# Projection phase: the gate projection split into three steps early in a group, and the newest convolution tap written by ScalarE out of PSUM

## The chip, the cores and the metric

One core of a Trainium2 chip runs the kernel. TensorE, VectorE, ScalarE and GpSimd each work through their own instruction queue in order, SyncE issues transfers, and semaphores tie the queues together. The metric is the device time of one execution, in microseconds (us).

## The reference

One inference step of a one-layer streaming encoder: 4096 prompt frames and 8 streams of 16 frames, model width 1024. What bears on the change is the first half of the mixer:

```
proj = rmsnorm(x) @ w_in                      # 3080 columns
x_lru, y_lru, qkv, z, b_logit, a_logit = columns of proj
xc    = causal_conv(x_lru, 4 taps) + lru_cb   # out[t] = sum over j of x[t-3+j] * w[j]
qkv_c = silu(causal_conv(qkv, 4 taps))
out_a = rglru(xc) * gelu(y_lru)               # gates r, i are sigmoids of two small matmuls on xc
beta  = sigmoid(b_logit)                      # 4 columns, one for each head
g     = -exp(a_log) * softplus(a_logit + dt_bias)
```

The gated delta rule, the output projection and a mixture of experts follow. The change doesn't touch them.

## The kernel before

`project_phase` handles 512 tokens (a group) at a time: eight groups of prompt tokens, the middle six in a loop, and a ninth of 128 tokens for the streams. Channels lie on the partitions, tokens along the free axis. The product runs in fp16 halves: each of 24 chunks of 128 columns is 8 x 3 matmuls of 128x512 into one of four PSUM banks (`pP`, L364).

`sequence()` writes down one list of steps, and every engine walks the same list and does its own share of each step. So a step that an engine waits in holds up all later steps of that engine. The steps:

- Y, X, Q, Z with a number: a chunk. TensorE makes it; ScalarE reads it from PSUM. Y (gelu) and Z (silu) are finished so. For X (4 chunks) and Q (12 chunks) ScalarE copies the bank into `win` (L465), and VectorE runs the 4-tap convolution: carry in (L617), a first tap as a product (L620 for X, with the bias; L622 for Q), carry out (L623), three multiply-adds (L626).
- S: silu of a finished Q on ScalarE, and its store. G, R, O: the gates of the recurrence (two matmuls `pG` on an X chunk, ScalarE functions, VectorE arithmetic), the scan, and the store.
- B: the 8 gate columns. TensorE does 96 small matmuls into `pB` (L388). VectorE adds the time bias (L664, `asum`). ScalarE takes the sigmoid, absolute value, exponential and logarithm with three function-table loads (L507 to L512). VectorE, which waits for that, ends with L668 and L670.
- D, E, H, T prepare the next group: VectorE spreads the row scales on a diagonal (D, L558), TensorE sums it over a matrix of ones (E, L347, `pR`), VectorE scales the eight blocks of `xT` (H, L568), ScalarE and VectorE cut them into fp16 halves (T: `h_hi` L423, `h_lo` L574). The next group's Y0 needs each of the halves. N takes the squares of the next tokens on ScalarE (L417).
- P: one of 60 pieces of expert weights for the later phase. A piece comes in by a transfer (256 KB), ScalarE rounds it (L435, `halves`), VectorE takes the remainder (L586), and a transfer writes it out (256 KB). SyncE issues, for each piece in list order, the write and then the load of the piece six places later. The six middle groups and a part of the eighth carry pieces; the first carries the splitting of `w_in` (`w_hi`, `w_lo`), chunk by chunk in the order of `wblocks`.

Before the change, B stands after Q9, D after the first piece behind Q10, and E after Q11 ahead of Z0. From Q3 on each chunk has three pieces.

Of the kernel before, what the change touches and what calls it, by code (L numbers as in the profile page):

```python
# [22 lines left out]
D = 1024  # L23
# [80 lines left out]
def sequence():  # L104

    free = iter(range(PER_GROUP))
    p = lambda n=1: [("P", next(free)) for _ in range(n)]
    w = iter([("W", k) for k in range(KD)])  # L110
    out = [("Y", 0)] + p() + [next(w), ("X", 0)] + p() + [next(w), ("Y", 1)] + p() + [next(w), ("X", 1), ("G", 0)] + p()
    out += [next(w), ("Y", 2)] + p(2) + [next(w), ("X", 2), ("R", 0), ("G", 1)] + p() + [next(w), ("Y", 3)] + p(2)
    out += [next(w), ("X", 3), ("O", 0), ("R", 1), ("G", 2)] + p() + [next(w), ("Q", 0)] + p()
    out += [("O", 1), ("R", 2), ("G", 3)] + p() + [("Q", 1)] + p() + [("S", 0), ("O", 2), ("R", 3)] + p()
    out += [("Q", 2)] + p(2) + [("S", 1), ("O", 3)] + p()
    tokens = {3: 0, 4: 1, 6: 2, 7: 3}
    for m in range(3, QC):
        out += [("Q", m)] + p() + [("S", m - 1)] + ([("N", tokens[m])] if m in tokens else [])
        out += [("B", 0)] * (m == 9) + [("D", 0)] * (m == 10) + [("E", 0)] * (m == 11) + p(2)
    out += [("Z", 0)] + p(2) + [("S", QC - 1)] + p(4) + [("Z", 1)] + p(3) + [("H", k) for k in range(4)] + p(3)  # L120
    out += [("Z", 2)] + [("H", k) for k in range(4, KD)] + [("T", k) for k in range(KD)] + [("Z", 3)] + p(4)
    assert next(free, None) is None and next(w, None) is None
    return out


def project_phase(nc, T, gb, cols):
# [6 lines left out]
    with ExitStack() as ctx:  # L133
# [51 lines left out]
        def col(name, n=0, w=1):  # L185
# [2 lines left out]
        last = f"Z{ZC - 1}"  # L188
        pe_names = [n for a, b in seq if a in "YXQZGB"
                    for n in ([f"{last}.{k}" for k in range(KD)] if f"{a}{b}" == last else (f"{a}{b}",))]  # L190
        act_names = [f"{a}{b}" for a, b in seq if a in "YXQZGRSB"]
        dve_names = [n for a, b in seq if a in "XGRQB" for n in (("Ba", "B") if a == "B" else (f"{a}{b}",))]
        pe_did = Steps(sem("project_pe"), pe_names)
        act_did = Steps(sem("project_act"), act_names)
        dve_did = Steps(sem("project_dve"), dve_names)
# [6 lines left out]
        h_did = Steps(sem("h_dve"), [f"L{k}" for k in range(KD)])  # L202

        wblocks = [(column[a] + m * P, P) for a, m in chunks]
        wblocks.insert(number["Q", 9] + 1, (IN - 2 * HEADS, 2 * HEADS))
        block_of = {c: wblocks.index((column[c[0]] + c[1] * P, P)) for c in chunks}
        block_of["B", 0] = number["Q", 9] + 1
        w_split = sem("w_split")
        w_hi_ready = sem("w_hi_ready")
        weights_in = [sem(f"weights_in{n}") for n in range(2)]  # L210
# [127 lines left out]
        def _(pe):  # L338
# [11 lines left out]
            def group(g, nt, following, first=False):  # L350
                N = nt * P
                for kind, m in seq:
# [17 lines left out]
                    elif kind == "E" and following:  # L370
                        spread(g + 1, following)
                    elif kind == "G":
                        if first and m == 0:
                            pe.wait_ge(gates_in, 16 * 4 * LC)
                        pe.wait_ge(*dve_did.at(f"X{m}", g))
                        pe.wait_ge(*act_did.at(f"G{(m - 1) % LC}", g, back=int(m == 0)))
                        for b in range(2):
                            ins = nc.tensor.matmul(pG[b][:, 0:N], gates[:, b, m, :], cv[:, m, 0:N], start=True, stop=True)
                        ins.then_inc(*pe_did.did(f"G{m}"))
                    elif kind == "B":  # L380
                        if first:
                            pe.wait_ge(w_split, block_of["B", 0] + 1)
                        pe.wait_ge(*dve_did.at("B", g, back=1))
                        pe.wait_ge(*act_did.at("B0", g, back=1))
# [25 lines left out]
        def _(act):  # L410
# [27 lines left out]
            def group(g, nt, stream, following, first=False, pieces=0):  # L438
# [5 lines left out]
                for kind, m in seq:  # L444
# [15 lines left out]
                    elif kind in "XQ":  # L460
# [4 lines left out]
                        nc.scalar.activation(window(c, 3, stream), shaped(pP[number[kind, m] % NPB][:, 0:N], stream),  # L465
                                             ACT.Copy, scale=PROJ).then_inc(*act_did.did(f"{kind}{m}"))
                    elif kind == "G":
                        act.drain()
                        act.wait_ge(*pe_did.at(f"G{m}", g))
# [24 lines left out]
                    elif kind == "Z":  # L494

                        act.wait_ge(*pe_did.at(f"{last}.{KD - 1}" if m == ZC - 1 else f"Z{m}", g))
                        slot = (QC + m) % 2
                        act.wait_ge(qo_out[slot], g * 128 + ((QC + m) // 2 + 1) * 16)
                        nc.scalar.activation(qo[:, slot, 0:N], pP[number[kind, m] % NPB][:, 0:N], ACT.Silu,
                                             scale=PROJ).then_inc(*act_did.did(f"Z{m}"))  # L500
                        act.drain()
                        store(QC + m, qo[:, slot, 0:N], qo_out[slot])
                    elif kind == "B":

                        act.wait_ge(*pe_did.at("B0", g))
                        act.wait_ge(*dve_did.at("Ba", g))
                        nc.scalar.activation(gb[:, bass.ds(g * GT, nt), 0:HEADS], pB[:, 0:nt, 0:HEADS], ACT.Sigmoid, scale=PROJ)  # L507
# [4 lines left out]
                        nc.scalar.activation(alog1[:, 0:nt], aexp[:, 0:nt], ACT.Ln, bias=1.0).then_inc(*act_did.did("B0"))  # L512

            for s in qo_out + halves_out:
                act.sem_inc(s, 16)
# [34 lines left out]
        def _(dve):  # L550
# [38 lines left out]
            def group(g, nt, stream, following, first=False, pieces=0):  # L589
                N = nt * P  # L590
                kept = carry_s if stream else carry
                for kind, m in seq:
# [10 lines left out]
                    elif kind in "XQ":  # L603
# [7 lines left out]
                        if c >= 8:  # L611
                            dve.wait_ge(*act_did.at(f"S{c - 8}", g))
                        elif c < 4:
                            dve.wait_ge(*act_did.at(f"S{QC - 4 + c}", g, back=1))
                        else:
                            dve.wait_ge(*pe_did.at(f"G{m}", g))
# [21 lines left out]
                    elif kind == "R":  # L638
# [12 lines left out]
                        else:  # L651
# [8 lines left out]
                    elif kind == "B":  # L660
                        dve.wait_ge(*pe_did.at("B0", g))
                        dtb = col("dtb", 0, HEADS).unsqueeze(1).to_broadcast([P, nt, HEADS])
                        neg = nea[:, :].unsqueeze(1).to_broadcast([P, nt, HEADS])
                        nc.vector.scalar_tensor_tensor(asum[:, 0:nt], pB[:, 0:nt, HEADS:], PROJ, dtb, ALU.mult, ALU.add  # L664
                                                       ).then_inc(*dve_did.did("Ba"))
                        dve.drain()
                        dve.wait_ge(*act_did.at("B0", g))
# [1651 lines left out]
```

## Time and profile before

| | |
|---|---|
| median of three runs | 3588.89 us (3588.49 to 3590.18) |
| profiled execution | 3602.5 us, span 3600.4 us |
| busy share: TensorE, VectorE, ScalarE | 86%, 59%, 43% |
| mean granted TensorE clock | 0.935 |
| matmuls of L364 in the projection phase | first 26.4 us, last 1284.7 us |
| one loop group, Y0 to Y0 | about 153 us |

The profile puts each engine's busy time and each idle stretch, with the event that ended it, on one time axis. The busy share mixes phases with different limits, so the projection phase is read by itself, and in it the group whose successor's Y0 starts at 632.12 us.

### The profile page before, as it was taken

The page shows a single profiled execution, that of the slowest core. Times are in us where ns is not written, and L with a number is a line of the kernel's source. Part 1 is how long each engine was busy: PE and PEld are TensorE (multiplying, and loading weights), DVE is VectorE, ACT ScalarE, POOL GpSimd, SP SyncE. Part 2 cuts the span into 40 slices and gives each one's busy share as a digit, 9 for nine tenths or more (in the row PEclk, how much of TensorE's full clock was granted, in tenths as well). Part 3 has the DMA queues.
Part 4 walks back from the last instruction along what each step waited for, and adds up shares of the span by engine and source line. Part 5 has one row for each costly group of instructions (what it writes and reads, how often), then busy time and mean ns, then how long its engine had stood idle before and what let it go on. Part 6 is the DMA issues. An engine that isn't in the chain of part 4 may idle for free. (4 is left out here: it accounts for less than half of the span.)

```text
span 3600.4 us, 65633 instructions
## 1 busy us (share of the span) xinstructions
PE 3106.1 (86%) x18226; PEld 1840.1 (51%) x18227; DVE 2124.0 (59%) x5319; ACT 1551.4 (43%) x3036; POOL 787.4 (22%) x1002
## 2 busy tenths in 40 slices
PE   7998898989889955999999999996799999999900
PEld 3443443434344555777777777664355555555500
DVE  5776867768687644676777776664333333333367
ACT  6565766657666522444444444441122222222222
POOL 0000000000000012455445554441111111111154
PEclk9999999999999966999999999998799999999955
DMA  5567769687785244545554454441677879984288
GB/s 157 159 218 275 270 237 321 216 314 256 244 296 203 86 128 116 153 137 154 150 154 134 138 156 138 129 118 56 212 257 249 284 242 320 321 276 155 99 312 312
DMA packets 497880, 733.44 MB, mean 204 GB/s; under 512 B 93425, under 2 KB 243537, under 8 KB 497361
## 3 DMA queue, kind: packets, MB, share of 16 engines
q1 hardware_dynamic: 414464, 497.94, 43.4%
q10 hardware_dynamic: 54288, 146.56, 10.4%
q0 software_dynamic: 28864, 86.09, 6.8%
q8 instruction: 85, 1.39, 0.2%
q14 instruction: 179, 1.46, 0.1%
HBM read 459.52 MB, written 270.92 MB: 203 GB/s over the span
## 5 line engine op out<-in xcount | busy, mean ns | idle before, releaser
L364 PE MATMUL pP<-h_hi,w_hi 128*128 128x512 f16 (+1 forms) x1728 | 628.2, 368 | 46.2 <-DVE h_lo L574 34.7
L364 PE MATMUL pP<-h_lo,w_hi 128*128 128x512 f16 (+1 forms) x1728 | 627.0, 367 | 0.0
L364 PE MATMUL pP<-h_hi,w_lo 128*128 128x512 f16 (+1 forms) x1728 | 625.7, 367 | 0.0
L1956 PE MATMUL ebank<-w_halves,rowsT_hi 128*128 x1568 | 486.5, 382 | 2.3 <-DVE rowsT_lo L2027 1.3
L626 DVE SCALAR_TENSOR_TENSOR cv<-win,cols_sb,cv 128x512 f32<-128x512 f32 (+1 forms) x432 | 305.4, 707 | 35.0 <-issue 0.4
L586 DVE SCALAR_TENSOR_TENSOR halves<-stage,halves 128x512 f16<-128x512 f32 x384 | 249.8, 685 | 94.3 <-ACT halves L435 94.0
L1956 PE MATMUL ebank<-w_halves,rowsT_lo 128*128 x784 | 299.4, 382 | 0.0
L364 PEld LDWEIGHTS pP<-h_hi,w_hi 128*128 128x128 f16 x1728 | 172.4, 100 | 244.2 <-issue 32.5
L435 ACT ACTIVATE halves<-stage 128x512 f16<-128x512 f32 x384 | 229.2, 621 | 107.9 <-DMA stage<-in_raw 75.6
L364 PEld LDWEIGHTS pP<-h_lo,w_hi 128*128 128x128 f16 x1728 | 172.4, 100 | 194.7 <-issue 23.3
L364 PEld LDWEIGHTS pP<-h_hi,w_lo 128*128 128x128 f16 x1728 | 172.2, 100 | 187.1 <-issue 10.5
L328 POOL TENSOR_TENSOR ss<-ss,eps 128x4 f32<-128x4 f32 (+1 forms) x9 | 3.7, 414 | 1153.3 <-ACT gy L417 1141.8
L1978 PE MATMUL ebank<-w_halves,guT_hi 128*128 x784 | 250.4, 381 | 2.4 <-DVE guT_lo L2033 2.4
L1956 PEld LDWEIGHTS ebank<-w_halves,rowsT_hi 128*128 128x128 f16 x1568 | 154.3, 98 | 183.1 <-issue 9.4
L1918 POOL DMA_INDIRECT rows<-h,idx x98 | 96.8, 988 | 687.7 <-PE ebank L1945 682.3
L2038 DVE SCALAR_TENSOR_TENSOR gu<-ebank,sil 128x256 f32<-128x256 f32 x98 | 41.6, 425 | 297.7 <-ACT sil L1997 297.7
L1997 ACT ACTIVATE sil<-ebank 128x256 f32<-128x256 f32 x98 | 37.6, 384 | 328.5 <-PE ebank L1956 328.5
L2043 DVE TENSOR_SCALAR yb<-ebank 128x512 f32<-128x512 f32 x98 | 67.8, 692 | 174.5 <-PE ebank L1978 174.5
L1978 PE MATMUL ebank<-w_halves,guT_lo 128*128 x392 | 149.3, 381 | 0.0
L2027 DVE SCALAR_TENSOR_TENSOR rowsT_lo<-ebank,rowsT_hi 128x512 f16<-128x512 f32 x196 | 126.4, 686 | 16.9 <-ACT rowsT_hi L1992 10.9
L1478 POOL DMA_INDIRECT table<-tid,offs x66 | 69.7, 1057 | 304.1 <-DVE offs L1730 278.3
L2001 ACT ACTIVATE guT_hi<-ebank 128x256 f16<-128x256 f32 x98 | 37.6, 384 | 224.7 <-ACTq L2011 223.6
(353 smaller groups left out, 6442.1 us busy)
## 6 DMA issues: line engine op xcount, KB each, us to landing
stage<-in_raw SPq DMA_DIRECT2D x384, 256.0 KB, 4.5
split<-halves SPq DMA_DIRECT2D x384, 256.0 KB, 4.3
w_halves<-split SPq DMA_DIRECT2D x32, 2048.0 KB, 11.3
y<-yb ACTq DMA_DIRECT2D x98, 512.0 KB, 7.2
ft<-mixin SPq DMA_DIRECT2D x33, 1280.0 KB, 8.3
mixin<-qo ACTq DMA_DIRECT2D x128, 256.0 KB, 3.9
w_halves<-split SPq DMA_DIRECT2D x32, 1024.0 KB, 6.1
xr<-in_x SPq DMA_DIRECT2D x33, 512.0 KB, 5.2
```

The lines of the kernel that those rows point to most:

```text
L364: ins = nc.tensor.matmul(pP[n % NPB][:, 0:N], w[:, k, c0:c0 + P], h[:, k, 0:N], start=(k + i == 0), stop=(k == KD - 1 and i == 2))
L435: nc.scalar.activation(halves[i % NHALF][:, 0, :], stage[:, i % NRAW, :], ACT.Copy, scale=W_SCALE).then_inc(hi_done, 1)
L586: nc.vector.scalar_tensor_tensor(halves[i % NHALF][:, 1, :], stage[:, i % NRAW, :], W_SCALE, halves[i % NHALF][:, 0, :], ALU.mult, ALU.sub ...
L626: ins = nc.vector.scalar_tensor_tensor(dst, window(c, j, stream), cw(j), dst, ALU.mult, ALU.add)
L1478: pool.indirect_dma_start(T["table"], bass.IndirectOffsetOnAxis(ap=offs[k][:, 0:1], axis=0), tid[:, 0:1], None).then_inc(ids_out, 16)
L1918: pool.indirect_dma_start(xb[p][:, :], None, T["h2"], bass.IndirectOffsetOnAxis(ap=idx[q][:, 0:1], axis=0)).then_inc(rows_in[p], 16)
L1956: ins = nc.tensor.matmul((M0, M1)[p][:, :], x[p][:, k, :], w[:, bass.ds(s, 1), k, half, :].rearrange("p a n -> p (a n)"), start=(k + i == ...
L1978: ins = nc.tensor.matmul((OA, OB)[h][:, :], g[p][:, k, :], down.rearrange("p a n -> p (a n)"), start=(k + i == 0), stop=(k == FE // P - 1 ...
L1997: nc.scalar.activation(sil[p][:, :], (M0, M1)[p][:, 0:FE], ACT.Silu, scale=PROJ).then_inc(*did(n))
L2027: nc.vector.scalar_tensor_tensor(part(xl), (TA, TB)[h][:, :], H_SCALE, part(xh), ALU.mult, ALU.subtract).then_inc(*did(n))
L2038: nc.vector.scalar_tensor_tensor(gu[p][:, :], (M0, M1)[p][:, FE:2 * FE], PROJ, sil[p][:, :], ALU.mult, ALU.mult).then_inc(*did(n))
L2043: nc.vector.tensor_scalar(yb[p][:, 512:], OB[:, :], OUT, None, ALU.mult).then_inc(*did(n))
```

## The change

Three things. First, B becomes three steps and moves from behind Q9 into the first half of the group. B (TensorE's 96 matmuls) stands after X1; U (VectorE's bias) after G1; V (ScalarE's functions) after G3; F (VectorE's end) after R3. The sigmoid is now a tanh with halved scale (V), made into a sigmoid by one more VectorE product in F. Second, ScalarE reads each X and Q bank twice: once into `win` as before, and once with the newest tap's weight into `cv` (Identity with a per-partition scale, and for X a per-partition bias). VectorE's first tap is gone; three multiply-adds remain. Those weights are scaled once at the start. Third, E moves behind Z0 and its two pieces. D stays.

```diff
-    out = [...] + [next(w), ("X", 1), ("G", 0)] + p()
+    out = [...] + [next(w), ("X", 1), ("B", 0), ("G", 0)] + p()
...
-        out += [("B", 0)] * (m == 9) + [("D", 0)] * (m == 10) + [("E", 0)] * (m == 11) + p(2)
-    out += [("Z", 0)] + p(2) + [("S", QC - 1)] + p(4) + [("Z", 1)] + ...
+        out += [("D", 0)] * (m == 10) + p(2)
+    out += [("Z", 0)] + p(2) + [("E", 0)] + [("S", QC - 1)] + p(4) + [("Z", 1)] + ...
...
-        wblocks.insert(number["Q", 9] + 1, (IN - 2 * HEADS, 2 * HEADS))
+        wblocks.insert(number["X", 1] + 1, (IN - 2 * HEADS, 2 * HEADS))
...
# ScalarE, X and Q
-    nc.scalar.activation(window(c, 3, stream), shaped(pP[...][:, 0:N], stream),
-                         ACT.Copy, scale=PROJ).then_inc(*act_did.did(f"{kind}{m}"))
+    made = pP[number[kind, m] % NPB][:, 0:N]
+    nc.scalar.activation(window(c, 3, stream), shaped(made, stream), ACT.Copy, scale=PROJ)
+    if 4 <= c < 8:
+        act.wait_ge(*pe_did.at(f"G{c - 4}", g))
+    nc.scalar.activation(cv[:, c % 4, 0:N], made, ACT.Identity, scale=col("cw", 4 * c + 3),
+                         bias=col("cb", m) if kind == "X" else 0.0).then_inc(*act_did.did(f"{kind}{m}"))
...
# ScalarE, B becomes V
-    act.wait_ge(*dve_did.at("Ba", g))
-    nc.scalar.activation(gb[...], pB[:, 0:nt, 0:HEADS], ACT.Sigmoid, scale=PROJ)
+    act.wait_ge(*dve_did.at("U0", g))
+    nc.scalar.activation(gb[...], pB[:, 0:nt, 0:HEADS], ACT.Tanh, scale=0.5 * PROJ)
...
# VectorE, X and Q: the waits for S and G go, and
-    nc.vector.tensor_scalar(dst, window(c, 0, stream), cw(0), None, ALU.mult)
     nc.vector.tensor_copy(kept[:, c], new)
-    for j in range(1, 4):
+    for j in (2, 1, 0):
...
# VectorE, F
+    beta = gb[:, bass.ds(g * GT, nt), 0:HEADS]
+    dve.wait_ge(*act_did.at("V0", g))
+    nc.vector.tensor_scalar(beta, beta, 0.5, 0.5, ALU.mult, ALU.add)
```

VectorE in a loop group, from Q9's convolution to Q11's, before (`halves` is a piece, `rg<-ident_sb,rs` is D):

```order
L626 SCALAR_TENSOR_TENSOR cv<-win,cols_sb,cv 128x512 x3
...
L664 SCALAR_TENSOR_TENSOR asum<-pB,cols_sb 128x16
...
L668 SCALAR_TENSOR_TENSOR aabs<-asum,alog 128x16
...
L670 TENSOR_TENSOR gb<-aabs,nea 128x4x4
...
L617 COPY win<-carry 128x3
L622 TENSOR_SCALAR cv<-win,cols_sb 128x512
L623 COPY carry<-win 128x3
...
L558 TENSOR_TENSOR rg<-ident_sb,rs 128x512
```

and now the place where F stands, between R3 (`oa<-oa,gy`) and Q2's convolution:

```order
L655 TENSOR_TENSOR oa<-oa,gy 128x512
...
L666 TENSOR_SCALAR gb<-gb 128x4x4
L667 SCALAR_TENSOR_TENSOR aabs<-asum,alog 128x16
...
L669 TENSOR_TENSOR gb<-aabs,nea 128x4x4
...
L593 SCALAR_TENSOR_TENSOR halves<-stage,halves 128x512
...
L618 COPY win<-carry 128x3
L620 COPY carry<-win 128x3
L623 SCALAR_TENSOR_TENSOR cv<-win,cols_sb,cv 128x512 x3
```

The three gate instructions have left the stretch between Q9 and D, and the product between the two small copies is gone from all 16 convolutions.

ScalarE in a loop group, from the last gate function of G3 to the next silu, before:

```order
L477 ACTIVATE th<-rg,sp 128x512
L435 ACTIVATE halves<-stage 128x512
...
L465 ACTIVATE win<-pP 128x512
...
L491 ACT_TABLE_LOAD
L491 ACTIVATE qo<-cv 128x512
```

and now, with V ahead of the piece and the second pass behind the copy of Q1:

```order
L481 ACTIVATE th<-rg,sp 128x512
...
L511 ACTIVATE gb<-pB 128x4x4
L512 ACTIVATE aabs<-asum 128x16
L514 ACTIVATE aexp<-aabs 128x16
L516 ACT_TABLE_LOAD
L516 ACTIVATE alog<-aexp 128x16
...
L466 ACTIVATE win<-pP 128x512
L469 ACTIVATE cv<-pP,cols_sb 128x512
...
L495 ACT_TABLE_LOAD
L495 ACTIVATE qo<-cv 128x512
```

One table load stands in V, where B had three; the load ahead of the next silu after B falls away too, since ScalarE then stays with silu from Q2's step to the group's end.

TensorE, the row-scale matmul E (`pR`) between the last matmul of Q11 (bank `pP3`) and the first of Z0 (bank `pP0`), before:

```order
L364 MATMUL pP3<-h_hi,w_lo 128x512
L345 ISA
L346 REGISTER_ALU
L347 MATMUL pR<-rg,ones 128x512
L356 REGISTER_ALU
L364 MATMUL pP0<-h_hi,w_hi 128x512
```

and now, behind the last matmul of Z0:

```order
L364 MATMUL pP0<-h_hi,w_lo 128x512
L345 ISA
L346 REGISTER_ALU
L347 MATMUL pR<-rg,ones 128x512
L356 REGISTER_ALU
```

It stands 24 matmuls, one chunk, later.

## Rows read from the trace of the kernel before

**Rows 1.** Longest waits in the trace, waiter <- releaser: us in total, times, longest

```profile
PE pR L347 <- DVE rg L558: 79.4, 8, 15.7
PE pP L364 <- DVE h_lo L574: 34.7, 7, 8.6
ACT halves L435 <- DMA stage<-in_raw: 75.6, 84, 3.6
```

**Rows 2.** Timeline of TensorE: gate matmuls, the row-scale matmul, the first chunk after it

```profile
start us, us, engine line op out<-in xcount [idle before <-releaser]
147.87 2.07 PE L347 MATMUL pR<-rg,ones 128*128 128x512 f32 x2 [3.27 <-DVE rg L558]
580.90 0.17 PE L388 MATMUL pB<-w_hi,h_hi 128*128 128x8 f16 x1
583.29 0.17 PE L388 MATMUL pB<-w_lo,h_hi 128*128 128x8 f16 x1
603.85 2.07 PE L347 MATMUL pR<-rg,ones 128*128 128x512 f32 x2 [10.01 <-DVE rg L558]
632.12 0.61 PE L364 MATMUL pP<-h_hi,w_hi 128*128 128x512 f16 x1 [4.40 <-DVE h_lo L574]
1280.41 0.29 PE L364 MATMUL pP<-h_hi,w_hi 128*128 128x128 f16 x1 [5.97 <-ACT win L465]
```

**Rows 3.** Timeline of VectorE in the same group, columns as above

```profile
548.33 0.68 DVE L642 TENSOR_TENSOR ig<-ig,th 128x512 f32<-128x512 f32 x1
551.96 0.16 DVE L617 COPY win<-carry 128x3 f32<-128x3 f32 x1
552.20 0.49 DVE L622 TENSOR_SCALAR cv<-win,cols_sb 128x512 f32<-128x512 f32 x1
552.60 0.16 DVE L623 COPY carry<-win 128x3 f32<-128x3 f32 x1
592.45 0.17 DVE L664 SCALAR_TENSOR_TENSOR asum<-pB,cols_sb 128x16 f32<-128x16 f32 x1
598.00 1.29 DVE L586 SCALAR_TENSOR_TENSOR halves<-stage,halves 128x512 f16<-128x512 f32 x2
603.03 0.68 DVE L558 TENSOR_TENSOR rg<-ident_sb,rs 128x512 f32<-128x512 f32 x1
```

**Rows 4.** Timeline of ScalarE in the same group, columns as above

```profile
537.35 0.69 ACT L471 ACTIVATE rg<-pG,half_b 128x512 f32<-128x512 f32 x1
544.89 1.28 ACT L481 ACT_TABLE_LOAD   x1 [1.22 <-DVE th L636]
546.18 0.63 ACT L481 ACTIVATE th<-th 128x512 f32<-128x512 f32 x1
592.74 1.28 ACT L507 ACT_TABLE_LOAD   x1 [4.30 <-DVE asum L664]
597.23 0.21 ACT L512 ACTIVATE alog<-aexp 128x16 f32<-128x16 f32 x1
629.33 4.27 ACT L423 ACTIVATE h_hi<-xT 128x512 f16<-128x512 f32 x8 [0.74 <-issue]
```

**Rows 5.** Busy time by stretch: engines, granted clock, DMA share, GB/s

```profile
core 0: us, PE busy (x) PEld busy (x) DVE busy (x) ACT busy (x) POOL busy (x), PEclk, DMA share, GB/s
485.00:638.00 153.00, 138.40 (x691) 62.74 (x688) 113.79 (x204) 98.08 (x153) 1.93 (x2) 0.96 0.76 268
550.00:629.33 79.33, 67.72 (x386) 31.27 (x384) 61.01 (x115) 45.79 (x80) 1.93 (x2) 0.94 0.95 338
550.00:590.00 40.00, 40.00 (x271) 19.42 (x270) 36.13 (x71) 24.25 (x44) 1.93 (x2) 1.00 1.01 368
590.00:603.00 13.00, 3.84 (x18) 1.57 (x16) 7.46 (x16) 9.46 (x15) 0.00 (x0) 0.80 0.70 240
570.00:580.00 10.00, 10.00 (x48) 4.50 (x46) 8.56 (x18) 6.78 (x12) 0.00 (x0) 1.00 1.05 407
620.00:632.00 12.00, 7.72 (x36) 3.33 (x34) 9.68 (x16) 6.82 (x13) 0.00 (x0) 1.00 1.05 386
```

More of the change, by code:

```diff
@@ L110, in sequence @@
     w = iter([("W", k) for k in range(KD)])
-    out = [("Y", 0)] + p() + [next(w), ("X", 0)] + p() + [next(w), ("Y", 1)] + p() + [next(w), ("X", 1), ("G", 0)] + p()
-    out += [next(w), ("Y", 2)] + p(2) + [next(w), ("X", 2), ("R", 0), ("G", 1)] + p() + [next(w), ("Y", 3)] + p(2)
+    out = [("Y", 0)] + p() + [next(w), ("X", 0)] + p() + [next(w), ("Y", 1)] + p() + [next(w), ("X", 1), ("B", 0), ("G", 0)] + p()
+    out += [next(w), ("Y", 2)] + p(2) + [next(w), ("X", 2), ("R", 0), ("G", 1)] + p() + [("U", 0)] + [next(w), ("Y", 3)] + p(2)
     out += [next(w), ("X", 3), ("O", 0), ("R", 1), ("G", 2)] + p() + [next(w), ("Q", 0)] + p()
-    out += [("O", 1), ("R", 2), ("G", 3)] + p() + [("Q", 1)] + p() + [("S", 0), ("O", 2), ("R", 3)] + p()
+    out += [("O", 1), ("R", 2), ("G", 3), ("V", 0)] + p() + [("Q", 1)] + p() + [("S", 0), ("O", 2), ("R", 3), ("F", 0)] + p()
     out += [("Q", 2)] + p(2) + [("S", 1), ("O", 3)] + p()
@@ L118, in sequence @@
         out += [("Q", m)] + p() + [("S", m - 1)] + ([("N", tokens[m])] if m in tokens else [])
-        out += [("B", 0)] * (m == 9) + [("D", 0)] * (m == 10) + [("E", 0)] * (m == 11) + p(2)
-    out += [("Z", 0)] + p(2) + [("S", QC - 1)] + p(4) + [("Z", 1)] + p(3) + [("H", k) for k in range(4)] + p(3)
+        out += [("D", 0)] * (m == 10) + p(2)
+    out += [("Z", 0)] + p(2) + [("E", 0)] + [("S", QC - 1)] + p(4) + [("Z", 1)] + p(3) + [("H", k) for k in range(4)] + p(3)
     out += [("Z", 2)] + [("H", k) for k in range(4, KD)] + [("T", k) for k in range(KD)] + [("Z", 3)] + p(4)
@@ L190, in project_phase @@
                     for n in ([f"{last}.{k}" for k in range(KD)] if f"{a}{b}" == last else (f"{a}{b}",))]
-        act_names = [f"{a}{b}" for a, b in seq if a in "YXQZGRSB"]
-        dve_names = [n for a, b in seq if a in "XGRQB" for n in (("Ba", "B") if a == "B" else (f"{a}{b}",))]
+        act_names = [f"{a}{b}" for a, b in seq if a in "YXQZGRSV"]
+        dve_names = [f"{a}{b}" for a, b in seq if a in "XGRQUF"]
         pe_did = Steps(sem("project_pe"), pe_names)
@@ L204, in project_phase @@
         wblocks = [(column[a] + m * P, P) for a, m in chunks]
-        wblocks.insert(number["Q", 9] + 1, (IN - 2 * HEADS, 2 * HEADS))
+        wblocks.insert(number["X", 1] + 1, (IN - 2 * HEADS, 2 * HEADS))
         block_of = {c: wblocks.index((column[c[0]] + c[1] * P, P)) for c in chunks}
-        block_of["B", 0] = number["Q", 9] + 1
+        block_of["B", 0] = number["X", 1] + 1
         w_split = sem("w_split")
@@ L382, in group @@
                             pe.wait_ge(w_split, block_of["B", 0] + 1)
-                        pe.wait_ge(*dve_did.at("B", g, back=1))
-                        pe.wait_ge(*act_did.at("B0", g, back=1))
+                        pe.wait_ge(*dve_did.at("F0", g, back=1))
+                        pe.wait_ge(*act_did.at("V0", g, back=1))
                         for t in range(nt):
@@ L464, in group @@
                         act.wait_ge(*dve_did.at(f"X{o}" if o < LC else f"Q{o - LC}", g, back=int(c < 4)))
-                        nc.scalar.activation(window(c, 3, stream), shaped(pP[number[kind, m] % NPB][:, 0:N], stream),
-                                             ACT.Copy, scale=PROJ).then_inc(*act_did.did(f"{kind}{m}"))
+                        made = pP[number[kind, m] % NPB][:, 0:N]
[4 more added lines that the diff above has]
+                                             bias=col("cb", m) if kind == "X" else 0.0).then_inc(*act_did.did(f"{kind}{m}"))
                     elif kind == "G":
@@ L502, in group @@
                         store(QC + m, qo[:, slot, 0:N], qo_out[slot])
-                    elif kind == "B":
+                    elif kind == "V":
                         act.wait_ge(*pe_did.at("B0", g))
-                        act.wait_ge(*dve_did.at("Ba", g))
-                        nc.scalar.activation(gb[:, bass.ds(g * GT, nt), 0:HEADS], pB[:, 0:nt, 0:HEADS], ACT.Sigmoid, scale=PROJ)
+                        act.wait_ge(*dve_did.at("U0", g))
+                        nc.scalar.activation(gb[:, bass.ds(g * GT, nt), 0:HEADS], pB[:, 0:nt, 0:HEADS], ACT.Tanh, scale=0.5 * PROJ)
                         nc.scalar.activation(aabs[:, 0:nt], asum[:, 0:nt], ACT.Abs)
@@ L511, in group @@
                         act.drain()
-                        nc.scalar.activation(alog1[:, 0:nt], aexp[:, 0:nt], ACT.Ln, bias=1.0).then_inc(*act_did.did("B0"))
+                        nc.scalar.activation(alog1[:, 0:nt], aexp[:, 0:nt], ACT.Ln, bias=1.0).then_inc(*act_did.did("V0"))
             for s in qo_out + halves_out:
@@ L532, in _ @@
             nc.scalar.activation(ln16[:, :], col("ln1", 0, KD), ACT.Copy, scale=H_SCALE)
+            act.drain()
+            newest = col("cw", 0, 4 * CC).rearrange("p (c j) -> p c j", j=4)[:, :, 3]
+            nc.scalar.activation(newest, newest, ACT.Copy, scale=PROJ)
             act.drain()
@@ L610, in group @@
                         dve.wait_ge(*act_did.at(f"{kind}{m}", g))
[L611 to L616, printed above, removed]
                         nc.vector.tensor_copy(old, kept[:, c])
                         dve.drain()
-                        if kind == "X":
-                            nc.vector.tensor_scalar(dst, window(c, 0, stream), cw(0), col("cb", m), ALU.mult, ALU.add)
-                        else:
-                            nc.vector.tensor_scalar(dst, window(c, 0, stream), cw(0), None, ALU.mult)
                         nc.vector.tensor_copy(kept[:, c], new)
-                        for j in range(1, 4):
+                        for j in (2, 1, 0):
                             dve.drain()
@@ L659, in group @@
                                                 ).then_inc(*dve_did.did(f"R{m}"))
-                    elif kind == "B":
+                    elif kind == "U":
                         dve.wait_ge(*pe_did.at("B0", g))
                         dtb = col("dtb", 0, HEADS).unsqueeze(1).to_broadcast([P, nt, HEADS])
+                        nc.vector.scalar_tensor_tensor(asum[:, 0:nt], pB[:, 0:nt, HEADS:], PROJ, dtb, ALU.mult, ALU.add
+                                                       ).then_inc(*dve_did.did("U0"))
+                    elif kind == "F":
                         neg = nea[:, :].unsqueeze(1).to_broadcast([P, nt, HEADS])
[L664 to L667, printed above, removed]
+                        beta = gb[:, bass.ds(g * GT, nt), 0:HEADS]
+                        dve.wait_ge(*act_did.at("V0", g))
+                        nc.vector.tensor_scalar(beta, beta, 0.5, 0.5, ALU.mult, ALU.add)
                         nc.vector.scalar_tensor_tensor(aabs[:, 0:nt], asum[:, 0:nt], 0.0, alog1[:, 0:nt], ALU.max, ALU.add)
@@ L670, in group @@
                         nc.vector.tensor_tensor(gb[:, bass.ds(g * GT, nt), HEADS:], aabs[:, 0:nt], neg, ALU.mult
-                                                ).then_inc(*dve_did.did("B"))
+                                                ).then_inc(*dve_did.did("F0"))
             nc.vector.memset(ones[:, :], 1.0)
```

## The prediction

> **What bounds the kernel now.** I read the list of waits first, for the engine that works longest: TensorE. In the projection phase its idle time has two places. It waits 79.4 us in eight visits for VectorE's diagonal D before the row-scale matmul E (the longest, 15.7, at the kernel's start), and 34.7 us in seven for `h_lo` before the first chunk of a group (8.6 at the start) [rows 1]. The timeline shows the two in one group: 10.01 us before E at 603.85, 4.40 us before Y0 at 632.12 [rows 2]. The first group has 3.27 us before E [rows 2]; 79.4 - 15.7 - 3.27 leaves 60.4 us for the six middle groups, 10.1 each, and the eighth, with few pieces, has none.
>
> Then the timelines of VectorE and ScalarE, to see why D is late. VectorE's step B begins at 592.45 with `asum`; its next piece begins at 598.00, so 5.55 us pass for three short instructions [rows 3]. In between ScalarE changes its function table and works until 597.44 [rows 4]. D begins at 603.03 [rows 3], and E follows it.
>
> Last, the stretches. Over a group VectorE is busy for 113.79 of 153 us, ScalarE for 98.08, the DMA engines for 0.76 of the time [rows 5]. But from 550 to 590 the DMA share is 1.01 at 368 GB/s, and from 620 to 632 it is 1.05 at 386. Only the 13 us around B, 0.70 at 240 GB/s, are slack [rows 5]. ScalarE waits 75.6 us in 84 visits for pieces to land [rows 1]. So behind the VectorE wait stands a second limit, the transfers of the pieces.
>
> **The change part by part**, in the group whose successor's Y0 starts at 632.12, times as in the trace of before.
>
> B on TensorE: 96 matmuls from 580.90 to 583.46, 2.5 us [rows 2]. They move, so TensorE's sum stays, but everything behind X1 comes 2.5 us later. The move of B's 8 columns among the weight blocks changes SyncE's order in the first group by one small transfer; I take nothing.
>
> E moves behind Z0. TensorE comes to E at 603.85 - 10.01 = 593.84. From the end of B (583.46) to there lie Q10 and Q11, so a chunk takes 5.19 us, and TensorE now comes to E at 599.0.
>
> ScalarE's second pass. The trace has no Identity with a per-partition scale. Nearest is the gate function that reads a PSUM bank with a per-partition bias, 0.69 us [rows 4]; the bounds are 0.63 (the square root, no such operand) and, with the same step of 0.06 once more for a second operand (X has two), 0.75 [rows 4]. I take 0.69; three passes differ by 0.2 us at either end. The third copy, Q0 and Q1 lie in the densest stretch of ScalarE, with the table loads of the recurrence. V adds what B cost, 592.74 to 597.44, less two of three loads: 4.70 - 2 x 1.28 = 2.1 us [rows 4]. So R3's square root, which ended at 546.81, ends later by 2.5 + 3 x 0.69 + 2.1 less the wait of 1.22 us ahead of it, which goes [rows 4]: 5.4, at 552.2. VectorE's R3, at 548.33 before [rows 3], waits for it and starts 3.9 us later. Queued behind it are Q2 and all later pieces.
>
> The Trainium skill, page ScalarE: Activation LUTs, section Rules for kernel authors, speaks against this part: additions and products belong on VectorE, not ScalarE. By it, 16 passes at 0.69 us for 16 products at 0.40 would lose 4.6 us a group; no run here shows that yet. The trace has ScalarE idle for 55 of 153 us, so I charge the pass only where ScalarE sets the pace.
>
> VectorE. The product costs 552.60 - 552.20 = 0.40 us from its start to the next [rows 3]. From Q2 to Q10 there are nine: 3.6 us. B's 5.55 us go. F adds three short instructions; by `asum`'s 0.17 us [rows 3] and the gaps between dependent ones, an estimate of 0.7 us. So D, at 603.03 before, starts at 603.03 + 3.9 + 0.7 - 3.6 - 5.55 = 598.5 and ends at 599.2, against TensorE's arrival at 599.0. The 10.01 us before E fall to nearly nothing. U stands early, where VectorE waits for TensorE's chunks.
>
> What is late next. From R3's start to the first `h_hi` of the next group at 629.33 [rows 4] the transfers carried 79.33 us x 338 GB/s = 26.8 MB [rows 5]. The same bytes must pass now; the pieces in this stretch start 3.9 us later, at 553.9, and T cannot begin before the last piece in front of it. At 368 GB/s (the longest full stretch) that is 72.9 us, at 386 (the tail) 69.5, at 407 (the best 10 us) 65.9 [rows 5]. T would begin at 626.8, 623.4 or 619.8. I take 386, since the tail has the same mix of pieces and stores. T is 5.9 us earlier, with 2.5 and 9.5 as ends. TensorE would be ready for Y0 at 599.2 + 2.07 (E) + 3 x 5.19 = 616.8, and must wait until 632.12 - 5.9 = 626.2. So the wait at Y0 grows from 4.4 to some 9 us, and 5.9 of the 14.4 us a group become time. The matmuls after a stall run at the lower of the two clock levels (the first lasts 0.61 us at 632.12, [rows 2]); a stall remains, so I count nothing for the clock.
>
> Sum: six groups x 5.9 = 35; the first group, without pieces, its 3.27 [rows 2]; in the stream group the wait of 5.97 us behind B goes [rows 2], of which its small passes take back about half, 3. Together 41 us. Profiled execution: 3602.5 - 41 = 3561. The median is 13.6 us below that execution: 3588.9 - 41 = 3548. The later phases do not change.
>
> **Rivals.**
> 1. The transfers leave room, and TensorE sets the pace. For it: 407 GB/s is possible, and the mean over the group is only 0.76. Against: share 1.01 over 40 us. Both waits would go, 10.01 + 4.40, less about 0.7 for a later G3: 13.7 x 6 + 6 = 88, so 3501.
> 2. The transfers bind at once. 368 GB/s is the most that 40 us showed, and the start is later. T at 626.8: 2.5 x 6 + 6 = 21, so 3568, and down to a few us of gain at a lower rate. For it: the share is already over 1. Against: the tail had 386. The Trainium skill, DMA: Bandwidth & Descriptors, section Where 436 GB/s comes from, gives about 358 GB/s as the limit of HBM for one core. By it the 26.8 MB need 74.9 us, the gain is 0.5 a group and the time 3580. The trace does not agree: 368 over 40 us, 407 over 10.
> 3. Slower: the turnaround of the ring of six buffers, not the rate, holds the pieces. A load waits in SyncE's queue for VectorE's end of the piece six places before; if that loop keeps the mean at 338 GB/s [rows 5] though the pause at B is gone, the stretch keeps its 79.33 us and only starts 3.9 us later. Then T is 3.9 later, 6 x 3.9 - 6 = 17, so 3606. It decides where the mean stays under 26.8 MB / 75.4 us = 355 GB/s. For it: ScalarE's denser chunk steps lengthen the loop. Against: 368 was held for 40 us while VectorE was slower than it will be.
> 4. D does not move forward, since ScalarE is behind in all Q steps and VectorE waits for its copies. Then E's move alone counts, 5.2 us at E, taken back by the late start: no change, 3589.
>
> **How the numbers follow.** Forecast 0.58, its own range 3523 (407 GB/s) to 3570 (368). Rival 1: 0.13. Rival 2 at the low rates, 3570 to 3585: 0.14. Rival 3: 0.11. Rival 4: 0.04. A measurement of this kernel tells 0.2%, 7 us, from no change. Faster: 0.58 + 0.13 + most of rival 2 = 0.83. Slower: rival 3 and the worst of 4, 0.11. Same: 0.06. The range 3505 to 3585 leaves out rival 3 and the better half of rival 1.
>
> **What would show it.** Right: the wait for D before E under 2 us in the middle groups; the wait for `h_lo` at Y0 grown to 7 to 11 us each; a DMA share over 1 without the pause, from Q2's step to T; period of a loop group about 147 us instead of 153; R3's square root followed closely by VectorE. Wrong: a Y0 wait that stays at 4 us or goes (rival 1); a long wait before E that remains, with VectorE waiting for `win` and `cv` (rival 4); a mean under 355 GB/s from R3 to T (rival 3).

## The result, and the profile after

| | before | after |
|---|---|---|
| median (range) | 3589.53 us (3588.49 to 3591.76) | 3570.22 us (3564.35 to 3571.19) |
| ratio to before, 95% interval | 1 | 0.9941 [0.9925, 0.9957] |
| profiled execution | 3602.5 us | 3569.6 us |
| first matmul of the next phase, in the profile | 1300.81 us | 1277.31 us |

The change makes the kernel 19 us faster by the medians (21 by the ratio); 41 were forecast. The two profiled executions differ by 33 us, but only 23.5 of it lie in the projection phase; the rest lies in later phases, which the change does not touch. So I read the phase alone: 4.5 us up to the second loop group's Y0 (325.22 to 320.69), 15.7 over five loop groups, 3.2 in the eighth group and the stream group together.

The waits of TensorE after, columns as in [rows 1]:

```profile
PE pP L364 <- DVE h_lo L581: 65.0, 7, 10.4
...
PE pR L347 <- DVE rg L565: 28.4, 7, 16.1
```

The wait before E fell from 79.4 to 28.4 us (16.1 of it at the kernel's start) and the wait at Y0 rose from 34.7 to 65.0: 51.0 less, 30.3 more. TensorE's timeline shows it for one loop group, from the Y0 at 469.88 to the next at 620.04, 150.16 us (153.10 before):

```profile
469.88 0.61 PE L364 MATMUL pP<-h_hi,w_hi 128*128 128x512 f16 x1 [9.75 <-DVE h_lo L581]
593.23 1.90 PE L347 MATMUL pR<-rg,ones 128*128 128x512 f32 x2 [1.95 <-DVE rg L565]
620.04 0.61 PE L364 MATMUL pP<-h_hi,w_hi 128*128 128x512 f16 x1 [8.46 <-DVE h_lo L581]
```

Against [rows 2], 10.01 + 4.40 us of waiting have become 1.95 + 8.46. VectorE of the same group, R3 and D as in [rows 3]:

```profile
544.69 0.69 DVE L639 TENSOR_TENSOR ig<-ig,th 128x512 f32<-128x512 f32 x1 [2.10 <-ACT th L485]
592.41 0.69 DVE L565 TENSOR_TENSOR rg<-ident_sb,rs 128x512 f32<-128x512 f32 x1
```

R3 now waits 2.10 us for ScalarE's square root; before, it waited for nothing. ScalarE ahead of that root, and at the group's end, as in [rows 4]:

```profile
520.04 0.77 ACT L469 ACTIVATE cv<-pP,cols_sb 128x512 f32<-128x512 f32 x1
...
540.88 0.63 ACT L495 ACTIVATE qo<-cv 128x512 f32<-128x512 f32 x1
541.70 0.34 ACTq L442 DMA_DIRECT2D mixin<-qo  x1
542.29 0.34 ACTq L442 DMA_DIRECT2D mixin<-oa  x1
542.73 1.28 ACT L485 ACT_TABLE_LOAD   x1 [1.22 <-DVE cv L623]
...
545.56 0.68 ACT L469 ACTIVATE cv<-pP,cols_sb 128x512 f32<-128x512 f32 x1
...
600.27 0.60 ACT L503 ACTIVATE qo<-pP 128x512 f32<-128x512 f32 x1 [3.12 <-DMA mixin<-qo]
617.27 4.27 ACT L423 ACTIVATE h_hi<-xT 128x512 f16<-128x512 f32 x8 [0.76 <-issue]
```

The second pass (L469) takes 0.77 with a bias and 0.68 without. The 1.22 us ahead of the table load is still there; in it lie two store issues. They stood there before, too, and VectorE's `th`, the releaser that [rows 4] names, ended at 543.99, ahead of the second of them:

```profile
543.30 0.69 DVE L636 SCALAR_TENSOR_TENSOR th<-rg,th 128x512 f32<-128x512 f32 x1
...
543.87 0.34 ACTq L442 DMA_DIRECT2D mixin<-qo  x1
544.45 0.34 ACTq L442 DMA_DIRECT2D mixin<-oa  x1
```

Z0's silu (L503) now waits 3.12 us for the store that last used its output buffer. And the stretches, as in [rows 5]: the group, R3's start, the middle, the tail, then R3 to D, D to T, and both together (T is the first `h_hi`):

```profile
469.88:620.04 150.16, 138.94 (x691) 62.82 (x691) 108.05 (x190) 103.56 (x167) 1.82 (x2) 0.95 0.76 274
543.00:553.00 10.00, 10.00 (x48) 4.58 (x47) 7.53 (x16) 8.64 (x14) 0.00 (x0) 1.00 0.61 196
553.00:593.00 40.00, 38.28 (x178) 17.12 (x176) 35.02 (x64) 29.50 (x55) 1.82 (x2) 1.00 1.05 403
593.00:623.00 30.00, 21.32 (x82) 8.76 (x83) 22.13 (x38) 17.35 (x32) 0.00 (x0) 0.79 1.03 380
544.69:592.41 47.72, 46.59 (x216) 20.93 (x214) 41.95 (x78) 35.87 (x64) 1.82 (x2) 1.00 0.96 362
592.41:617.27 24.86, 18.35 (x74) 7.72 (x74) 16.99 (x29) 12.85 (x24) 0.00 (x0) 0.86 1.04 378
544.69:617.27 72.58, 64.94 (x290) 28.65 (x288) 58.94 (x106) 48.72 (x87) 1.82 (x2) 0.95 0.99 367
```

VectorE's work fell by 5.8 us a group, ScalarE's rose by 5.5, and the transfers run above a share of 1 from 553 on, without the pause of [rows 5].

### The profile page after: what moved, and what is told of

It reads as the page before. It is cut to its first block and busy times, and to the rows that moved or that the text cites. A ratio compares the mean times of both kernels' runs of the same rounds, so it can differ in the third digit from the quotient of the medians.

```text
span 3567.9 us, 65471 instructions
## 1 busy us (share of the span) xinstructions
PE 3096.7 (87%) x18226; PEld 1835.7 (51%) x18227; DVE 2077.5 (58%) x5184; ACT 1595.9 (45%) x3154; POOL 795.2 (22%) x1002
## 3 DMA queue, kind: packets, MB, share of 16 engines
q10 hardware_dynamic: 54288, 146.56, 10.4%
## 5 line engine op out<-in xcount | busy, mean ns | idle before, releaser
L2026 DVE SCALAR_TENSOR_TENSOR rowsT_lo<-ebank,rowsT_hi 128x512 f16<-128x512 f32 x196 | 126.5, 686 | 16.5 <-ACT rowsT_hi L1991 10.4
```

The source lines that it names most:

```text
L2026: nc.vector.scalar_tensor_tensor(part(xl), (TA, TB)[h][:, :], H_SCALE, part(xh), ALU.mult, ALU.subtract).then_inc(*did(n))
```

## The experiments

Theory T: once D comes earlier, the transfers of the pieces set the time, not TensorE's wait before E. The first expectations mean the whole stretch from R3 to T by it; the runs narrow it to the tail, D to T. Its rivals stand with each run. Ratios are to the kernel before as it was timed beside each run (medians of 3588.5 to 3591.1 us), so where runs of different rows are compared the ratios count, and the medians are the rougher measure. The first table has the medians, and the mean period of the five loop groups (T to T) in each profile.

| run | median us | ratio [95%] | period us |
|---|---|---|---|
| before | 3588.5 to 3591.1 | 1 | 153.2 |
| changed | 3570.2 | 0.9941 [0.9925, 0.9957] | 150.1 |
| e1 before, E behind Z0 | 3581.8 | 0.9989 [0.9974, 1.0004] | 153.2 |
| e2 gates alone | 3576.4 | 0.9963 [0.9950, 0.9977] | 150.9 |
| e3 tap alone | 3574.5 | 0.9958 [0.9945, 0.9971] | (e12) 151.0 |
| e4 changed, no token rows | 3557.8 | 0.9916 [0.9903, 0.9929] | 147.5 |
| e5 changed, buffers in turn | 3570.5 | 0.9954 [0.9939, 0.9968] | 150.2 |
| e6 changed, pieces early | 3546.5 | 0.9879 [0.9863, 0.9894] | 147.6 |
| e7 changed, tap in part | 3571.9 | 0.9948 [0.9934, 0.9961] | 149.6 |
| e8 = e6 + e5 | 3522.2 | 0.9808 [0.9795, 0.9822] | 142.9 |
| e9 before + e8's two edits | 3560.1 | 0.9923 [0.9909, 0.9937] | 147.6 |
| e10 = e8, E ahead of Z0 | 3540.5 | 0.9871 [0.9854, 0.9887] | 145.4 |
| e11 = e8 + e7 | 3513.0 | 0.9797 [0.9781, 0.9813] | 139.7 |

The second table cuts one loop group at three starts of the timelines: VectorE's R3, VectorE's D, ScalarE's T. Groups of one run differ in a cut by up to 3 us, so the last column has D to T as the mean of the five loop groups.

| | Y0 to R3 | R3 to D | D to T | T to Y0 | D to T, five groups |
|---|---|---|---|---|---|
| before | 69.31 | 54.70 | 26.30 | 2.79 | 26.2 |
| forecast | 73.2 | 46.3 | 24.9 | 2.8 | |
| e1 E behind Z0 | 70.70 | 55.24 | 24.42 | 2.78 | 24.7 |
| e2 gates alone | 72.39 | 49.37 | 26.34 | 2.79 | 26.1 |
| e12 tap alone | 69.97 | 52.25 | 26.08 | 2.80 | 25.7 |
| changed | 74.81 | 47.72 | 24.86 | 2.77 | 24.8 |
| e4 no token rows | 74.74 | 45.47 | 24.23 | 2.80 | 24.5 |
| e6 pieces early | 77.28 | 47.45 | 19.05 | 5.51 | 19.0 |
| e7 tap in part | 73.27 | 48.16 | 25.82 | 2.79 | 24.8 |
| e8 | 74.18 | 47.53 | 15.31 | 4.52 | 15.5 |

### e1: E's move alone

```diff
-    ... [("D", 0)] * (m == 10) + [("E", 0)] * (m == 11) + p(2)
-    out += [("Z", 0)] + p(2) + [("S", QC - 1)] + ...
+    ... [("D", 0)] * (m == 10) + p(2)
+    out += [("Z", 0)] + p(2) + [("E", 0)] + [("S", QC - 1)] + ...
```

> Only the third part: E stands behind Z0, gates and taps as in the kernel before. Theory T (transfers): from R3 to the first h_hi the pieces' transfers set the time; TensorE's wait before E falls from 10 us by one chunk, to about 5, but h_hi comes at most 1 us earlier, since the transfers are full at the group's end; the wait at Y0 grows from 4.4 to 8 or 9 us. Time 0 to 6 us under the kernel before. Rival P (TensorE's waits are the loss): what goes before E is time, 5 us in each of six groups, 25 to 30 us faster, the wait at Y0 unchanged.

In the loop groups there is no difference: the period is 153.2 us as before. TensorE's timeline of e1:

```profile
596.93 2.07 PE L347 MATMUL pR<-rg,ones 128*128 128x512 f32 x2 [5.38 <-DVE rg L558]
623.32 0.61 PE L364 MATMUL pP<-h_hi,w_hi 128*128 128x512 f16 x1 [7.27 <-DVE h_lo L574]
```

The window of the group that ends there, columns as in [rows 5]:

```profile
470.18:623.32 153.14, 140.29 (x690) 63.22 (x691) 114.18 (x205) 98.18 (x154) 1.96 (x2) 0.95 0.76 268
```

The wait before E halved (10.01 to 5.38). Of the 4.63 us it lost, Y0's wait took 2.87 and TensorE's own work 1.8: 140.29 us instead of 138.50 for the same matmuls, at a granted clock of 0.95 instead of 0.96. A shorter wait before E is worth nothing by itself in a loop group: T stands. The medians are 8 us apart, though the ratio's interval takes in 1; in the profile 7.7 us of the phase go ahead of the second loop group's Y0 (325.22 to 317.48), most of it in the first group, which has no pieces.

In e1 D to T is 24.7 us in the mean, as in the changed kernel, and D comes as much later. So the shorter tail goes with E's place behind Z0, not with an earlier D.

### e2, e3, e12: the gates alone, the tap alone

e2 is the changed kernel with L469 taken out, the tap on VectorE again, and E behind Q11. e3 and e12 are one kernel: the second pass stays, B, U, V and F stand together behind Q9, E behind Q11.

> Only the first part: B, U, V, F early; taps on VectorE and E after Q11 as before. Theory T: B's 5.5 us of VectorE go, R3 starts about 4 us later (B's 2.5 us on TensorE, V's 2 us on ScalarE), so D is 1.5 to 2 us earlier in the group, the wait before E about 8 us, and the pause of the transfers around B is gone: h_hi 2 us earlier, 10 to 15 us faster in all. Rival S (ScalarE's list sets the pace): the 4 us at R3 stay, time the same as before or up to 5 us slower.

> Only the second part: the newest tap on ScalarE; gates after Q9 (in three pieces, one behind the other) and E after Q11 as before. Theory T: VectorE's steps are 0.4 us shorter, R3 about 2 us later through three more passes of ScalarE; the transfers from Q3 to B are full already, so D gains at most 1 us and the pause around B stays; 0 to 8 us faster. Rival S: ScalarE, 16 passes of 0.6 us longer in a group, holds VectorE up, 5 to 15 us slower. Rival V (VectorE sets the pace): 9 x 0.4 less 2 us in each group, about 10 us faster, with the wait before E near 8 us.

> One look at the part with the tap on ScalarE alone, for its trace. VectorE's pace (each of nine products of 0.40 us from Q2 to Q10 brings D forward, 3.6 us, less what ScalarE's passes delay R3): the wait before E falls from 10 to 7 to 8.5 us, Y0's wait stays at 4 to 5, period 150 to 151. Theory T in its narrow form (the transfers hold the time from R3's start on): the wait before E falls but the Y0 wait grows by the same, period about 152.5.

Both parts pay alone, 13 and 15 us; T gave the tap 0 to 8 and falls there. The two and e1's 4, which is not clear of noise, would make 32 us, and the whole change gives 21 by the same ratios: together the parts are worth less than alone (in the period of a loop group 2.3, 2.3 and nothing, against 3.1). TensorE in e12:

```profile
593.40 2.07 PE L347 MATMUL pR<-rg,ones 128*128 128x512 f32 x2 [7.21 <-DVE rg L565]
621.47 0.54 PE L364 MATMUL pP<-h_hi,w_hi 128*128 128x512 f16 x1 [4.12 <-DVE h_lo L581]
```

Only the wait before E shrank, from 10 to 7.2; Y0's stayed near 4, so T moved with D. The second table says why: D to T is 26.2, 26.1 and 25.7 us in before, e2 and e12. With E ahead of Z0 the tail is a length behind D, not a fixed end. What brings D forward is then paid in full, and the rates of R3 to D matter less than the forecast had it.

### e4: the changed kernel without the token rows

```diff
-                if 14 <= n < 14 + GT:
-                    token_load(n - 14, 1)
...
-                    elif kind == "R" and i == LC - 1:
-                        for t in range(min(2, n)):
-                            token_load(t, g + 1)
...
-                        norm(m, tok[m % 2], g + 1)
+                        norm(m, tok[m % 2], g + 1, w_hi[:, 0, 0:D])
```

The squares are taken of other numbers, and so are the row scales and all that follows; the work on the engines stays.

> The changed kernel without the loads of the next group's token rows (four of 512 KB in a group, all in the stretch from R3 to h_hi); N takes the squares of a tile that is there already, so the row scales, and all that follows, are of other numbers. Nothing else moves, and N never waited for these loads. Theory T: 2.1 MB of 26.6 MB fewer, at 380 to 403 GB/s 5.2 to 5.5 us a group; h_hi that much earlier, the wait at Y0 from 9 to about 4 us, 25 to 33 us faster than the changed kernel, near 3540. Rival S: the order and lengths on ScalarE are as they were, so less than 5 us faster, with the wait at Y0 still 8 us and a DMA share well under 1.

12 us faster than the changed kernel by the medians, 9 by the ratios, between the two. But the wait at Y0 did not fall to 4 us, as T had it: it is 9.0 to 10.7. What went is the wait before E, from about 2 us to 0.43 or less. TensorE's Y0 of e4:

```profile
614.35 0.61 PE L357 MATMUL pP<-h_hi,w_hi 128*128 128x512 f16 x1 [9.51 <-DVE h_lo L573]
```

The windows of e4 from R3 to D and from D to T:

```profile
541.85:587.32 45.47, 45.47 (x212) 20.63 (x211) 41.51 (x78) 35.96 (x65) 1.82 (x2) 1.00 0.90 330
587.32:611.55 24.23, 17.52 (x80) 7.69 (x77) 16.99 (x29) 12.42 (x22) 0.00 (x0) 0.92 1.04 391
```

With fewer bytes R3 to D takes 45.47 instead of 47.72 us at a share of 0.90; the tail stays full at 1.04 and loses only 0.6. So from R3 to D the transfers held 2.2 us a group, less than half of the 5.2 to 5.5 that T put on these bytes. In the tail e4 takes nothing away: the token rows are loaded ahead of D.

### e5, e6, e8: the tail

e5 gives S11, Z0, Z1, ... the two output buffers in turn (S10 and Z0 shared one). e6 moves nine pieces out of the tail:

```diff
# e5, ScalarE, S and Z
-                        slot = m % 2
+                        turn = m + (m == QC - 1)
+                        slot = turn % 2
...
-                        slot = (QC + m) % 2
+                        turn = QC + m - (m == 0)
+                        slot = turn % 2
# e6
-    out = [("Y", 0)] + p() + [next(w), ("X", 0)] + p() + [next(w), ("Y", 1)] + p() + ...
+    out = [("Y", 0)] + p(3) + [next(w), ("X", 0)] + p(3) + [next(w), ("Y", 1)] + p(3) + ...
-    ... [("S", QC - 1)] + p(4) + [("Z", 1)] + p(3) + [("H", k) for k in range(4)] + p(3)
+    ... [("S", QC - 1)] + p(2) + [("Z", 1)] + p() + [("H", k) for k in range(4)] + p()
```

> The changed kernel with the two output buffers of ScalarE taken in turn: Z0 takes the buffer of S9 and not that of S10 just ahead of it, S11 that of S10, Z1 that of Z0. In the changed kernel ScalarE waits 3.1 us at Z0 for S10's store and 1.7 us ahead of Z1. Theory T (transfers set the time from Q3 to h_hi): the DMA share is 1.03 there, so the waits only turn into waits for pieces; h_hi at most 0.5 us earlier, 0 to 5 us faster than the changed kernel. Rival R (ScalarE's stops at the stores hold the pieces up): 3 to 4.8 us in each of six groups, 18 to 29 us faster, the wait at Y0 down from 9 to about 5 us.

> The changed kernel with nine of the 60 pieces moved from behind Z0 into the steps Y0 to Y3, where the transfers have room (under 200 GB/s). Theory T: nine of the pieces that stand between Q11 and the next Y0 go, six of them ahead of T: 3.1 MB, at 380 to 403 GB/s 7.8 to 8.3 us a group, until TensorE's own time is the limit; the wait at Y0 falls from 9 to under 3 us, a group takes 142 to 144 us, 35 to 48 us faster than the changed kernel, near 3528. Rival S (the lists of ScalarE and VectorE, not the transfers): the same work stands in the lists only earlier, where it delays X3 and R3; less than 10 us faster.

> The pieces moved early and the output buffers in turn, both on the changed kernel. Theory T: with 3.1 MB fewer ahead of h_hi the transfers are no longer full at the group's end, so the waits for the stores count by themselves only if h_hi is still late; 40 to 55 us faster than the changed kernel, TensorE's waits under 3 us a group. Rival R: the waits at the stores are the rest, so this is 15 us or more faster than the pieces moved alone.

e5 alone does nothing, as T had it: the waits at the stores turn into waits for pieces. ScalarE's list of waits has them for the changed kernel, then for e5:

```profile
ACT halves L435 <- DMA stage<-in_raw: 67.5, 95, 1.4
```

```profile
ACT halves L435 <- DMA stage<-in_raw: 100.3, 137, 2.0
```

e6 gains 24 us (22 by the ratios), less than T's 35 to 48, and its wait at Y0 is still 4.7 to 7.8 us (under 3 forecast). D to T lost 5.8 us, but T to Y0 took 2.7 back. ScalarE in e6 shows what is left to gain:

```profile
601.22 0.60 ACT L503 ACTIVATE qo<-pP 128x512 f32<-128x512 f32 x1 [3.14 <-DMA mixin<-qo]
609.14 0.60 ACT L503 ACTIVATE qo<-pP 128x512 f32<-128x512 f32 x1 [3.23 <-DMA mixin<-qo]
```

Two waits for stores, in series with fewer pieces. In e8 both are gone, and the two edits together are worth 48 us, twice e6, as rival R had it. The windows of e8, group and tail:

```profile
459.01:600.55 141.54, 136.61 (x691) 62.27 (x691) 108.11 (x190) 103.43 (x168) 1.82 (x2) 0.99 0.80 290
580.72:596.03 15.31, 14.50 (x65) 6.54 (x66) 11.58 (x21) 8.80 (x16) 0.00 (x0) 1.00 1.05 399
```

ScalarE late in that tail:

```profile
590.91 0.63 ACT L435 ACTIVATE halves<-stage 128x512 f16<-128x512 f32 x1 [1.10 <-DMA stage<-in_raw]
```

D to T is 15.3 us instead of 24.9, while VectorE's and ScalarE's work in the group is as in the changed kernel (108.05 and 103.56). T expected transfers that are no longer full there, and that falls: the share is 1.05, and ScalarE still waits for pieces. The tail is shorter because it carries less, 15.31 us x 399 GB/s = 6.1 MB instead of 24.86 x 378 = 9.4.

### e7, e11: less ScalarE work ahead of R3

X0 to X3, Q0 and Q1 take their newest tap on VectorE again.

```diff
+                        if c >= 6:
...
+                            ins = nc.scalar.activation(cv[:, c % 4, 0:N], made, ACT.Identity, scale=col("cw", 4 * c + 3))
```

> The changed kernel with the newest tap back on VectorE for X0 to X3, Q0 and Q1, and on ScalarE from Q2 on. ScalarE has three passes of 0.6 us fewer between X3 and R3, VectorE, which waits 2.1 us ahead of R3, three products more. Theory T: the piece-rich stretch starts 1.5 us earlier in a group and takes as long; 6 to 10 us faster than the changed kernel, VectorE's wait ahead of R3 under 1 us. Rival: the start does not matter, as the transfers from Q3 on cannot go faster than about 403 GB/s and their bytes ahead of h_hi fix its time; within 3 us of the changed kernel.

> The changed kernel with pieces early and buffers in turn, and the newest tap on VectorE for X0 to X3, Q0 and Q1, so that ScalarE has six passes fewer ahead of R3's square root. Theory T (VectorE's start at R3 now counts, since the tail is free): D comes 1.5 to 3 us earlier, the 2 us before E shrink to about 0: 6 x 1 to 2 us, 3510 to 3516. Rival (the six added products on VectorE take back what the earlier start gives, as with the tail in place): 3518 to 3526.

In e7 R3 comes 1.5 us earlier in this group (73.27), 0.9 in the mean of the five, and R3 to D takes 0.4 back. The period is 0.5 us shorter and the medians show no gain, so T's 6 to 10 us fall. On top of e8 the same edit brings the period from 142.9 to 139.7 in one profile of each, and gives 9 us by the medians but 4 by the ratios, whose intervals overlap for the most part. That the earlier start counts only where the tail is short is what the two profiles say; the times alone do not show it. e11 has the lowest median of all runs.

### e9, e10: the change and E's move with the tail shortened

> The kernel before, with the two edits that took the changed kernel down by 48 us: nine pieces moved from behind Z0 to Y0 to Y3, and the output buffers in turn. Theory T (D's wait and the transfers of the tail are two limits in series; the change lifts the first, these edits the second): without the change the wait of 10 us before E stays and only the 4.4 us at Y0 shrink to about 2.5, so 2 us a group, 3575 to 3580, and the change is worth about 55 us on top of these edits. Rival (the tail alone sets the time, the change's gates and tap matter little): the edits are worth 40 to 50 us here too, 3540 to 3550.

> The changed kernel with pieces early and buffers in turn, and E again behind Q11, ahead of Z0. Theory T: the transfers no longer bind, so TensorE's order does; the wait before E grows from 2 us by one chunk, 5.2, and the 2.5 us of wait at Y0 take part of it back: 2.7 us in each of six groups, 16 us slower than 3522, so about 3538. Rival (the tail still sets the time): no change, 3518 to 3526, with the Y0 wait going down as the wait before E goes up.

e9 gains 28 us without the change, between both expectations; the change on top is worth 38 by the medians, 41 by the ratios (55 forecast). TensorE's E rows of e9, then of e10:

```profile
591.99 2.07 PE L347 MATMUL pR<-rg,ones 128*128 128x512 f32 x2 [10.76 <-DVE rg L560]
```

```profile
587.09 2.07 PE L347 MATMUL pR<-rg,ones 128*128 128x512 f32 x2 [6.96 <-DVE rg L567]
```

In e9 the wait for D stays whole and Y0 waits for nothing. The period lost 5.6 us, more than the 4.4 that waited there; the windows from T to T, of before and of e9, show the rest in TensorE's own time:

```profile
476.22:629.33 153.11, 138.50 (x690) 62.88 (x690) 113.90 (x205) 98.08 (x153) 1.93 (x2) 0.96 0.76 267
```

```profile
464.16:611.49 147.33, 136.37 (x692) 62.47 (x690) 113.76 (x205) 97.83 (x153) 1.81 (x2) 0.97 0.79 278
```

2.1 us less for the same matmuls, at a granted clock of 0.97 instead of 0.96. e10 is 18 us slower than e8 by the medians, 23 by the ratios (T said 16): E's place, worth nothing in e1's loop groups, counts once the tail is short.

## Why the prediction was right, and half in size

- **Direction and mechanism** were right: two limits, of which the change lifts the first and meets the second. The wait before E is 1.9 to 2.3 us in the loop groups (under 2 forecast), Y0's 8.3 to 10.4 (7 to 11 forecast), the share above 1 with no pause behind 553.
- **The tail**: 623.4 - 598.5 = 24.9 us from D to T was forecast, 24.86 measured, and that is in part luck. D and T both came 3.0 us later than forecast, so their distance says little of the rate behind it, and e1 has this tail with E's move alone. The forecast let T follow from the bytes since R3 at 386 GB/s, 71.2 us from R3 (552.2) to T. It took 72.58 us, a mean of 367 GB/s.
- **Rival 2** (368 GB/s, 3568 us) comes nearer to the time, 3570, than the forecast does. But its mechanism, that 368 is the most the transfers hold, falls: 553 to 593 ran at 403 and the tail at 378, and the mean is lower because the 10 us from 543 on ran at 196. The Trainium skill, DMA: Bandwidth & Descriptors, section Where 436 GB/s comes from, puts the limit of HBM for one core at about 358 GB/s; 403 over 40 us disagree, and the measurement decides.
- **D's step was mis-sized**: forecast 4.5 us earlier, counted from Y0, measured 1.5 (124.01 to 122.53). Two terms make it. First, "less the wait of 1.22 us ahead of it, which goes": it stayed. Without that term gates alone are 2.5 + 2.1 - 1.52 (R3's old slack behind the root, 548.33 - 546.81) = 3.1 late at R3, measured 3.1 (e2); the tap alone 2.07 - 1.52 = 0.55, measured 0.66 (e12); both 5.2, measured 5.5. That the two store issues make it is read from their rows; no run takes them away. Second, R3 to D: forecast 8.45 us shorter, measured 6.98. The engines could (9.2 in e4, without the token rows); with them the transfers did not let them.
- **A loop group** so gained 1.48 (D) + 1.44 (tail) = 2.9 us, not 5.9; over the phase 23.5 by the profile, not 41. The stream group's 3 was right (3.2 with the eighth).
- **The second pass** was right, 0.68 without a bias and 0.77 with one for 0.69. The Trainium skill, ScalarE: Activation LUTs, section Rules for kernel authors, advises against it; the trace disagrees with the rule here. The tap alone gains 15 us, since it shortens VectorE's way from R3 to D (54.70 to 52.25 in e12) and delays R3 by 0.66.
- **The clock** was charged nothing: right for the change (138.50 to 138.94 us of TensorE work), but TensorE's work falls by 2.1 us a group in e9, where Y0's stall goes, and rises by 1.8 in e1, where it grows.
- **Rival 1** (3501 us) is what e8 and e11 come near to, but they need a shorter tail for it. **Rival 3** falls (a mean of 367 GB/s from R3 to T, above its 355). **Rival 4** in part: D moved by a third of what was due.

## What to carry to other kernels

Cut a period at the starts of the steps that hand over, and price a change in each cut: gain ahead of D was paid in full only while the cut behind D kept its length. Two limits in series hide each other's worth: the store buffers were worth nothing until the pieces had moved, and then as much as the pieces. When a profile names a releaser that ended before the wait did, look for the instructions between, here store issues, before writing that the wait will go.

## What the runs showed of the hardware

- One core's transfers held 403 GB/s for 40 us, reads and writes mixed, at a share of 1.05.
- ScalarE's pass over a PSUM bank of 128x512 with a per-partition scale takes 0.68 us, with a bias too 0.77; two store issues cost ScalarE 1.22 us between two functions, booked as a wait for VectorE.
- Y0's first matmul takes 0.61 us at a granted clock of 0.50, the lower level, after 8.46 us of waiting in the changed kernel, and 0.39 at 1.00, the upper, after 2.35 in e8. The length of that wait alone does not decide it: 0.61 came after 2.88 in e11, 0.39 after 3.71 in before. The windows of the two first matmuls, the changed kernel's and e8's, and e8's matmul:

```profile
620.04:620.50 0.46, 0.46 (x2) 0.18 (x3) 0.46 (x1) 0.46 (x2) 0.00 (x0) 0.50 1.05 405
```

```profile
600.55:601.00 0.45, 0.45 (x3) 0.20 (x3) 0.45 (x1) 0.45 (x2) 0.00 (x0) 1.00 1.04 401
```

```profile
600.55 0.39 PE L364 MATMUL pP<-h_hi,w_hi 128*128 128x512 f16 x1 [2.35 <-DVE h_lo L583]
```
